# Two slots of raw weights and four of split weights, split three units ahead, in a two-block transformer kernel on one core

## What is computed

```python
ada = (c @ w_ada + b_ada)                       # 1024 x 6144
shift1, scale1, gate1, shift2, scale2, gate2 = jnp.split(ada, 6, axis=-1)
h = rmsnorm(x, g_norm1) * (1.0 + scale1) + shift1
proj = h @ w_in                                 # q, k, v of both attentions, indexer, two gates
...                                             # forgetting attention, sparse (top 64) attention
merged = sigmoid(gate_fox) * (y_fox @ w_branch_fox) + sigmoid(gate_dsa) * (y_dsa @ w_branch_dsa)
x = x + gate1 * (merged @ w_out)
h2 = rmsnorm(x, g_norm2) * (1.0 + scale2) + shift2
x = x + gate2 * (jnp.square(jax.nn.relu(h2 @ w_mlp1)) @ w_mlp2)
x = rmsnorm(x, g_final)
# second block, per layer: a mixer (convolution, or differential attention) and attention over the memory
x = x + concat([main, mo]) @ w_o[l]
x = x + jnp.square(jax.nn.relu(rmsnorm_2(x, norm_mlp[l]) @ w_up[l])) @ w_down[l]
```

## Time and profile before

| | |
|---|---|
| median of 3 runs | 1191.41 us (1191.03 to 1191.85) |
| profiled execution | 1190.21 us, of it 1188.4 us span of the trace |
| granted TensorE clock, mean | 0.947 of full speed |
| TensorE busy | 1109.9 us (93%) |
| VectorE, ScalarE, GpSimd busy | 641.9, 534.8, 356.4 us |
| mean load on the DMA queues | 51.4% of 16 engines, 166 GB/s |

### The profile page before, as it was taken

One profiled execution on the slowest core, in us unless ns is written; L12 is line 12 of the kernel. 1 busy time (PEld: TensorE's weight loads), 2 busy tenths in 40 slices (PEclk: granted clock), 3 DMA queues, 4 the chain that ended last, 5 costly groups with the idle time before them and its releaser, 6 DMA issues.

```text
span 1188.4 us, 20203 instructions
## 1 busy us (share of the span) xinstructions
PE 1109.9 (93%) x8758; PEld 1083.8 (91%) x8758; DVE 641.9 (54%) x833; ACT 534.8 (45%) x737; POOL 356.4 (30%) x198
## 2 busy tenths in 40 slices
PE   7989999999899999959998999999998668999998
PEld 7989989889899999959998999998997558999998
DVE  2767766455575744464744544444646644644443
ACT  3337756664356544334344443443534432544441
POOL 3233726514054622111013221231531121323111
PEclk9879989989899999979998999998999688999999
DMA  9857755844547655524354655564442103655640
GB/s 321 242 188 221 246 178 156 270 143 142 178 138 252 210 191 189 192 71 142 107 179 129 202 189 190 178 200 142 142 142 72 36 19 98 203 178 180 187 166 36
DMA packets 167716, 197.39 MB, mean 166 GB/s; under 512 B 5283, under 2 KB 139852, under 8 KB 167500
## 3 DMA queue, kind: packets, MB, share of 16 engines
q1 hardware_dynamic: 167628, 196.11, 51.4%
HBM read 195.03 MB, written 1.06 MB: 165 GB/s over the span
## 4 chain that ended last, share of the span: by engine, by line
PE 75%; DVE 10%; ACT 7%; DMA 3%; POOL 2%; issue 2%; DVEq 0%; SPq 0%; ACTq 0%; POOLq 0%
PE bank L459 74%; DVE w_lo L1433 3%; DMA ada_raw<-in_w_ada 3%; ACT w_hi L974 2%; ACT ada_raw L964 2%; ACT probs L1020 1%; POOL ada_raw L1312 1%; POOL root L1288 1%; DVE fresh L1469 1%; DVE fresh L1475 0%; DVE ada_late L1749 0%; DVE y_tok L1527 0%; DMA qk<-in_mem 0%; POOL head_bias L1350 0%; DVE big L1631 0%
## 5 line engine op out<-in xcount | busy, mean ns | idle before, releaser
L1433 DVE TENSOR_TENSOR w_lo<-w_raw,w_hi 128x2048 fp32r<-128x2048 f32 x158 | 386.5, 2449 | 301.3 <-ACT w_hi L974 300.4
L459 PE MATMUL bank<-h_hi,w_hi 128*128 128x256 f32 x1328 | 383.6, 294 | 14.6 <-ACT h_hi L983 10.2
L459 PE MATMUL bank<-h_hi,w_lo 128*128 128x256 f32 x1328 | 378.9, 290 | 0.0
L974 ACT ACTIVATE w_hi<-w_raw 128x2048 fp32r<-128x2048 f32 x158 | 301.2, 1907 | 132.7 <-PE bank L459 132.6
L459 PE MATMUL bank<-h_lo,w_hi 128*128 128x256 f32 x1328 | 345.1, 285 | 0.0
L459 PE MATMUL bank<-u_hi,w_hi 128*128 128x256 f32 x1056 | 301.6, 289 | 8.8 <-DVE xT L1826 4.6
L459 PE MATMUL bank<-u_hi,w_lo 128*128 128x256 f32 x1056 | 298.9, 287 | 0.0
L459 PE MATMUL bank<-u_lo,w_hi 128*128 128x256 f32 x1056 | 285.5, 286 | 0.0
L459 PEld LDWEIGHTS bank<-h_hi,w_hi 128*128 128x128 f32 x1328 | 265.6, 200 | 18.5 <-issue 13.5
L1281 POOL TENSOR_TENSOR u_lo<-fresh,u_hi 128x512 fp32r<-128x512 f32 x68 | 153.6, 2262 | 425.2 <-ACT u_hi L983 425.0
L459 PEld LDWEIGHTS bank<-h_hi,w_lo 128*128 128x128 f32 x1328 | 265.3, 200 | 0.0
(11 more groups left out here) (188 smaller groups left out, 968.0 us busy)
## 6 DMA issues: line engine op xcount, KB each, us to landing
w_raw<-in_w_mlp SPq DMA_DIRECT2D x32, 1024.0 KB, 5.4
w_raw<-in_w_up SPq DMA_DIRECT2D x32, 1024.0 KB, 5.5
w_raw<-in_w_down SPq DMA_DIRECT2D x32, 1024.0 KB, 5.1
w_raw<-in_w_in SPq DMA_DIRECT2D x21, 1024.0 KB, 5.8
ada_raw<-in_w_ada SPq DMA_DIRECT2D x20, 1024.0 KB, 8.1
w_raw<-in_a_w_in SPq DMA_DIRECT2D x10, 1024.0 KB, 5.1
w_raw<-in_w_o SPq DMA_DIRECT2D x8, 1024.0 KB, 5.2
w_raw<-in_w_kv SPq DMA_DIRECT2D x6, 1024.0 KB, 4.9
```

The costliest lines, as they stand in the source:

```text
L459: return pe.matmul(dst, lhsT, rhs, start=start, stop=stop, skip_group_check=True)
L974: act.activation(w_hi[:, n % PARTS_RING, :], w_raw[:, slot_of[n], :], ACT.Copy).then_inc(hi_w, 1)
L1433: dve.tensor_tensor(w_lo[:, n % PARTS_RING, :], w_raw[:, slot_of[n], :], w_hi[:, n % PARTS_RING, :].bitcast(F32), ALU.subtract).then_inc(l ...
```

## The change

Three constants change. With them every written `split_w(n + AHEAD)` and every wait that names RING or PARTS_RING changes. The fixed numbers in the startup are adapted at three places. Nothing is computed differently.

```diff
-RING = 4
-PARTS_RING = 3
-AHEAD = 2
+RING = 2
+PARTS_RING = 4
+AHEAD = 3
...
@@ scalar engine
             split_w(11)
+            split_w(12)
             evac(9, flat(qk, 6, 8))
...
-            split_w(N_DSA + AHEAD, late=True)
+            split_w(N_DSA + AHEAD)
...
                 split_h(J_FOX + q, u_hi, 2 * q)
-            scale_ada(ADA_LATE[N_DSA + AHEAD])
...
@@ vector engine
             pick_eight()
-            for n in range(9, 14):
+            split_w(9)
+            for n in range(10, 15):
                 split_w(n)
                 pick_eight()
```

## The result

The changed kernel takes 1348.33 us in the median of four runs (1346.76 to 1351.11). The kernel before, run beside it on the same chip, takes 1191.22 us (1188.78 to 1191.85). The ratio is 1.1329, with a 95% interval from 1.1311 to 1.1347: slower, as forecast, and 2.3 us above the predicted 1346. The profiled execution took 1347.74 us, its span 1346.0 us, which is 157.6 more than before.

What follows compares the result with a forecast made beforehand. TensorE bounds the MLPs, while ScalarE sets the pace in the first 137 us. Stage losses of 145.6 us plus 10 us for the clock, added to the profiled 1190.2 us, gave 1346 us, range 1275 to 1385.

Steps and rivals of the forecast that it cites:

- start, units 0 to 5: Startup: the load of unit 6 waits for `w_lo` of unit 4 and lands after ScalarE wants it, 5.0 us.
- units 6 to 14: Pieces a8 to a12: longer ScalarE waits, plus scaling and one more `w_hi` ahead of a taking out, 54.6 us.
- units 16 to 24: Pieces a13 to a17: four waits of 10.8 us and part of a13's, less earlier waits, 38.8 us.
- sparse attention: Pieces a18 and a19 wait and are scaled ahead of `copy_turned` in the second and fourth pair, 20.9 us.
- norm ahead of MLP 0: Piece a20 lands late and is scaled before the norm's last square, with nothing else running: 13.8 us.
- MLP 0: Pieces a21 to a23: the lead absorbs the first wait, the other two stick out by about 6.2 each, 12.5 us.
- clock: New TensorE stalls bring half-clock stretches; three taken as uncovered, 10 us, between 0 and 25.
- The wait for pieces: ScalarE's wait for the condition's pieces rises from 28.9 to about 165 us, in 16 places of 10 to 13.
- the lead pays: Rival: the waits for `w_lo` go, up to 16.9 us, and no piece comes late: 1174 us, chance 0.02.
- Partly hidden: Rival: lead and ScalarE's slack swallow waits after the first attention; 67 us remain, so 1257 us, chance 0.10.
- The weights' loop starves too: Rival: landings grow past 7.4 us and each unit pays half the excess; at 9 us, 1470 us, chance 0.04.
- Two slots suffice: Rival: the condition's pieces land in time as most did before, leaving 1191 us, chance 0.03.

Runs made afterwards that it cites:

- e1: Changed kernel with the condition's pieces queued right behind unit m instead of m + 2 (LOAD_LAG 0): 1200.53 us, ratio 1.0092.
- e3: Kernel before, its slots and lead kept, with the condition's pieces queued later, behind unit m + 4 (LOAD_LAG 4): 1337.45 us, ratio 1.1237.
- e4: Kernel before with only its raw slots lowered from four to two (RING 2): 1343.14 us, ratio 1.1278.
- e5: Kernel before with the condition's pieces queued earlier, behind unit m + 1 (LOAD_LAG 1): 1185.35 us, ratio 0.9955.
- e2: Changed kernel with the condition's pieces queued behind unit m + 1 instead of m + 2 (LOAD_LAG 1): 1261.24 us, ratio 1.0603.
- e8: Kernel before with only its raw slots lowered from four to three (RING 3): 1249.67 us, ratio 1.0497.
- e6: Changed kernel with pieces queued behind unit m and five scalings (units 12, 14, 24, 26, 28) moved behind the following taking out or copy: 1191.43 us, ratio 1.0011.
- e10: Kernel before with the scaling of units 12, 22, 24 and 26 moved behind the taking out of PSUM or copy_turned: 1184.57 us, ratio 0.9950.

## Why the prediction was right

The forecast case came true, with the sum made against the profiled execution of 1190.2 and a result of 1347.7 in the profiled one. Term by term, by the end of the products above:

| step | predicted us | measured us |
|---|---|---|
| start, units 0 to 5 | 5.0 | 4.2 (`w_hi` of unit 6 ended at 85.36 instead of 81.12) |
| start and units 6 to 14 together | 59.6 | 62.8 at unit 12, 54.7 at unit 14 |
| units 16 to 24 | 38.8 | 42.1 from unit 14 to 22 |
| sparse attention | 20.9 | 26.2 from unit 22 to 33 |
| norm ahead of MLP 0 | 13.8 | 13.2 |
| MLP 0 | 12.5 | 18.1 |
| behind | 0 | 3.2 |
| clock | 10 | within the rows above |

The mechanism is the one that was forecast, and e1, e3 and e4 show it. That the total came within 2 us is partly luck. No row is off by more than 5.6 us, but their errors have both signs. And TensorE's idle time grew by 132.6 us and its busy time by 25.0, where the sum had 145.6 for the waits and 10 for the clock.

- *The wait for pieces* was forecast at about 165 us in 16 places of 10 to 13, and is 183.8 in 16 of 8.6 to 13.9, eleven of them between 10 and 13. The two short ones, 8.6 and 9.0, are a13 and a14, which are scaled a few instructions later than the others. Where VectorE was free, one took nearly the 10.8 that the sum of its parts said: 10.36, 10.43, 10.48 us. Most of the others are longer because VectorE came to `w_lo` late (at a20 1.6 us after the end of `w_hi`, 438.67 to 440.26) or had that of another unit and a pick first, as in the rows of a11. I had counted this for a10 to a12 only. So "each piece is issued 2.7 us after the end of `w_hi`" came true for eight of the sixteen (2.8 us); for the other eight it was 3.8 to 5.6. The sum over all sixteen is 12.8 us more than 16 x 2.7. The time to landing, 7.9 us in the median, was as good as the 8.1 of the earlier trace rows.
- *Units 6 to 14* were followed along ScalarE's order, and this is the step where that paid: scaling and one more `w_hi` do stand ahead of the taking out. At unit 12 the loss is 62.8 us, but 8.1 of it come back by unit 14, among the pairs of heads; the sum had nothing of that. a13 then costs its share ahead of unit 15.
- *The norm* is the plainest term, 13.8 against 13.2: one wait, one scaling, nothing beside them. e3 and e4 show no loss there, since without the third unit of lead a20 is scaled behind the square.
- *MLP 0* was sized too small. TensorE was idle for 3.51, 3.45 and 5.39 us, 12.35 together, as much as forecast; but I had let the lead eat the first of the three, and it did not. (The sum there has 23.5 us of TensorE for four units, which would make 5.8 and not 6.2 of 29.3; at 5.79 us a unit it is 23.2, and 6.2 is right.) Rows of ScalarE:

```profile
484.73 1.92 ACT L974 ACTIVATE w_hi<-w_raw 128x2048 fp32r<-128x2048 f32 x1 [2.63 <-DMA w_raw<-in_w_mlp]
498.87 3.31 ACT L964 ACTIVATE ada_raw<-ada_raw,vec 128x256 f32<-128x256 f32 x8 [12.22 <-DMA ada_raw<-in_w_ada]
...
512.40 1.92 ACT L974 ACTIVATE w_hi<-w_raw 128x2048 fp32r<-128x2048 f32 x1 [5.10 <-DMA w_raw<-in_w_mlp]
514.22 0.58 ACT L1155 ACTIVATE fresh<-bank 128x512 f32<-128x512 f32 x1
516.21 1.92 ACT L974 ACTIVATE w_hi<-w_raw 128x2048 fp32r<-128x2048 f32 x1 [1.41 <-DMA w_raw<-in_w_mlp]
...
528.49 3.31 ACT L964 ACTIVATE ada_raw<-ada_raw,vec 128x256 f32<-128x256 f32 x8 [10.36 <-DMA ada_raw<-in_w_ada]
...
559.05 3.31 ACT L964 ACTIVATE ada_raw<-ada_raw,vec 128x256 f32<-128x256 f32 x8 [11.52 <-DMA ada_raw<-in_w_ada]
```

  The `w_hi` ahead of the first wait had itself waited 2.63 us for raw weights, so the lead was not yet built up. The loop of four units, from one scaling to the next, took 29.6 and 30.6 us; forecast was 29.3. The rest of the 18.1, 5.8 us, is about what TensorE's stretches at half clock behind these idle times account for.
- *The clock.* The granted clock was 0.50 of full speed (1.2 of 2.4 GHz) in 283 us of the span, before in 126. TensorE was busy in 150.4 us of these, before in 95.1. Half of the difference, 27.6 us, is what full speed would have saved, and it accounts for the 25.0 us by which its busy time grew. How much of it is felt can't be read one by one; the 10 us taken for it lie inside the stage rows, whose sum is 157.5 against 145.6.
- *Behind unit 49* nothing was forecast, and 3.2 us came. The idle time ahead of unit 124 is 4.60 us as before.
- *Gains from the lead* were put at 1 us at most. None is to be seen: the waits for `w_lo` rose by 11.2 us (22.4 against 11.2), as I read it because after a late piece the splits run late as well. The prediction's 16.9 us in eight places counts three idle times twice (PE and PEld); it should read 11.2 in five, and the rival "the lead pays" 1180 in place of 1174.
- *The range.* Its upper end adds up to 1380 (1346 + 19 + 15), not to 1385; nothing hangs on it.

**The rivals.** "Partly hidden" put 1257 us; there was little cover for the waits of the changed kernel (154.9 us more of waiting, 157.6 us more of time), though those of the kernel before were mostly covered, that of 9.4 us for a8 included (e5). "The weights' loop starves too" fell: in MLP 0 `w_hi` waits 40.0 us in 14 places for raw weights, but in MLP 1 and MLP 2 only 8.7 and 8.4 us in four places each, and TensorE is not idle for them. "The lead pays" fell: pieces came late, and no run with three units of lead is faster than its nearest run with two (the changed kernel against e4, e2 against e8, e6 against e10). "Two slots suffice" is false of this kernel and true of its weights: e6 has two slots and 1191.43 us. The advice of the Trainium skill (Trainium Kernel Development and Optimization, Best Practices) to double-buffer thus holds here for the data that the slots carry, and fails for what is queued behind them; e1 and e6 against the changed kernel show the difference, 146 us and 156 us.

## What to carry to other kernels

A queue that issues in order makes every load wait for the slot of the load ahead of it. When the number of slots is lowered, look first at what else stands in that queue: it is released later by as many steps, and must be queued that much earlier (LOAD_LAG goes with RING). Ask for each load which event releases it, which instruction needs it, and whether anything lies between the two; more lead doesn't help where both move together, and may cost where the release hangs on something that doesn't move. And place a wait that may be long behind what another engine is waiting for: in e10 this alone gains 5.8 us on the kernel before.

## What the runs showed of the hardware that was not expected

- A piece issued 0.4 us behind a load of weights landed after 7.6 to 8.7 us in fourteen of the sixteen places of the kernel after (a8 and a10 took 10.1 and 9.9), though the DMA engines moved only 142 GB/s in the mean there; the medians of the other kernels lie between 7.8 and 8.3. The loads of weights took 5.4 in the median.
- VectorE's `w_lo`, 2.29 us in the median, took 3.06 us in the row of a11 and up to 6.01 in the kernel before. There, the 89 of 158 that had no work of GpSimd beside them all took 2.30 us or less; each of the 21 longer ones had GpSimd at work beside it, the 15 over 3 us nearly all along. In e6 GpSimd's two sums took 7.74 us while VectorE made two `w_lo` (196.00 to 206.19); in e3 two such sums took 3.73 us in a stretch in which VectorE was idle (its next `w_lo` began at 154.41 after 14.99 us of idle time). The row of e3:

```profile
150.17 3.73 POOL L1312 TENSOR_TENSOR ada_raw<-ada_raw 128x1024 f32<-128x1024 f32 x2 [21.99 <-ACT ada_raw L964]
```

  That the two engines hold each other up is my reading of the rows; no run measured it by itself. The Trainium skill (GPSIMD Engine Reference, Specifications) says that GpSimd shares its way into SBUF with VectorE, with contention where an instruction of VectorE has two inputs from there, as `w_raw - w_hi` has; these rows agree.
- 157 us more at half the granted clock go with 25.0 us more of busy time: TensorE was busy in only 150.4 of the 283 us. So the mean granted clock (0.895 against 0.947) is a sign of the stalls and not a cause of their length.
